# Three weight slabs in place of five for the self-attention keys and values, with the second copies of the keys made by DMA

## What is computed

```python
h = rmsnorm(x, p['norm_mix_pre'][i])
proj = h @ p['w_in_attn'][j]
q, k, v, cq = jnp.split(proj, [Q_WIDTH, Q_WIDTH + KV_WIDTH, Q_WIDTH + 2 * KV_WIDTH], axis=-1)
k = k.reshape(b, l, N_KV_HEADS, HEAD_DIM)      # 3 heads of 64
v = v.reshape(b, l, N_KV_HEADS, HEAD_DIM)
...
s = jnp.einsum('bcqkgd,bcskd->bckgqs', qb, kb).astype(jnp.float32) / math.sqrt(HEAD_DIM)
```

## Time and profile before

| | |
|---|---|
| median of 3 runs | 1857.19 us (1854.53 to 1864.68) |
| the profiled execution | 1860.35 us, span 1858.5 us, mean granted TensorE clock 0.986 |
| TensorE busy | 1757.7 us, 95% of the span |
| VectorE, ScalarE, GpSimd busy | 791.6, 698.7, 749.0 us |
| memory projections of both layers | until 74.6 us |
| slabs 16 to 20 (keys and values) | 74.6 to 106.9 us |
| transposes of the values | 106.9 to 110.1 us |
| four query slabs | 110.1 to 135.8 us |

### The profile page before, as it was taken

One profiled execution on the slowest core, in us unless ns is written; L12 is line 12 of the kernel. 1 busy time (PEld: TensorE's weight loads), 2 busy tenths in 40 slices (PEclk: granted clock), 3 DMA queues, 4 the chain that ended last, 5 costly groups with the idle time before them and its releaser, 6 DMA issues.

```text
span 1858.5 us, 31140 instructions
## 1 busy us (share of the span) xinstructions
PE 1757.7 (95%) x13115; PEld 1683.0 (91%) x13115; DVE 791.6 (43%) x1534; ACT 698.7 (38%) x1318; POOL 749.0 (40%) x438
## 2 busy tenths in 40 slices
PE   6999999999999999999899999989999999999996
PEld 5997887998999999998798989877898999999996
DVE  5427777315412112126856676755504411212124
ACT  6416666324312121224455555553514312122221
POOL 1231121242736354451345555553232745445451
PEclk9999999999999999999899999998999999999998
DMA  5521210121222222221222222212121222222221
GB/s 217 191 80 52 69 64 30 57 87 51 91 84 87 80 80 85 86 80 46 84 88 87 78 94 83 92 60 102 46 80 58 91 80 80 86 85 80 80 87 67
DMA packets 47659, 153.68 MB, mean 83 GB/s; under 512 B 8257, under 2 KB 10017, under 8 KB 47265
## 3 DMA queue, kind: packets, MB, share of 16 engines
q1 hardware_dynamic: 40144, 140.59, 22.3%
q10 hardware_dynamic: 7376, 11.10, 1.8%
HBM read 145.21 MB, written 6.47 MB: 82 GB/s over the span
## 4 chain that ended last, share of the span: by engine, by line
PE 81%; DVE 8%; ACT 4%; POOL 3%; issue 2%; DMA 1%; SPq 0%; POOLq 0%; DVEq 0%; ACTq 0%
PE ps L959 70%; DVE mix L1459 1%; PE ps L942 1%; PE ps L1123 1%; PE ps L1094 1%; POOL sq L2075 1%; ACT dec L856 1%; DVE x L1462 1%; PE ps L1175 1%; PE ps L1112 1%; PE ps L1198 1%; PE ps L1332 1%; POOL w_lo L1954 1%; DVE big_lo L1403 1%; DMA raw<-in_slabs 1%
## 5 line engine op out<-in xcount | busy, mean ns | idle before, releaser
L1954 POOL TENSOR_TENSOR w_lo<-raw,w_hi 128x1024 fp32r<-128x1024 f32 x225 | 547.9, 2437 | 753.3 <-ACT w_hi L472 661.2
L959 PE MATMUL ps<-big_hi,w_hi 128*128 128x288 f32 x3552 | 781.1, 301 | 7.9 <-POOL w_lo L1954 3.2
L959 PE MATMUL ps<-big_lo,w_hi 128*128 128x288 f32 x3552 | 758.9, 297 | 7.7 <-DVE big_lo L1403 7.7
L959 PE MATMUL ps<-big_hi,w_lo 128*128 128x288 f32 x3552 | 765.1, 296 | 0.0
L959 PEld LDWEIGHTS ps<-big_hi,w_hi 128*128 128x128 f32 x3552 | 574.9, 190 | 17.6 <-issue 12.5
L959 PEld LDWEIGHTS ps<-big_lo,w_hi 128*128 128x128 f32 x3552 | 571.3, 189 | 13.1 <-DVE big_lo L1403 12.2
L959 PEld LDWEIGHTS ps<-big_hi,w_lo 128*128 128x128 f32 x3552 | 575.9, 189 | 0.1
L472 ACT ACTIVATE w_hi<-raw 128x1024 fp32r<-128x1024 f32 x242 | 255.3, 1057 | 489.7 <-DMA raw<-in_slabs 479.8
L1713 DVE TENSOR_TENSOR mix<-ps,mix 128x576 f32<-128x576 f32 x62 | 47.0, 758 | 307.3 <-PE ps L959 307.3
L1701 DVE SCALAR_TENSOR_TENSOR relu<-ps,rstd 128x576 f32<-128x576 f32 x60 | 45.4, 757 | 280.2 <-PE ps L959 280.2
L1997 POOL TENSOR_TENSOR hid<-relu 128x576 f32<-128x576 f32 x64 | 98.6, 1543 | 157.6 <-DVE relu L1701 157.5
(11 more groups left out here) (197 smaller groups left out, 1644.6 us busy)
## 6 DMA issues: line engine op xcount, KB each, us to landing
raw<-in_slabs SPq DMA_DIRECT2D x242, 512.0 KB, 3.4
row<-acs_prompt ACTq DMA_DIRECT2D x16, 384.0 KB, 3.3
bias<-in_alibi SPq DMA_DIRECT2D x12, 256.0 KB, 2.7
x<-in_x SPq DMA_DIRECT2D x2, 1152.0 KB, 8.6
out_h<-state ACTq DMA_DIRECT2D x4, 384.0 KB, 2.6
out_y<-x SPq DMA_DIRECT2D x2, 576.0 KB, 2.8
kms<-in_mk SPq DMA_DIRECT2D x2, 512.0 KB, 5.2
vms<-in_mv SPq DMA_DIRECT2D x2, 512.0 KB, 6.3
```

Source lines behind the costliest of these rows:

```text
L959: ins = pe.matmul(ps[:, bank + h, 0:hi_c - lo_c], w[:, s % RING, kt], a[:, k0 + kt, lo_c:hi_c], start=start, stop=stop, skip_group_check=True)
L1954: pool.tensor_tensor(w_lo[:, s % RING], raw[:, s % RING], w_hi[:, s % RING].bitcast(F32), ALU.subtract).then_inc(lo_done, 1)
```

## The change

The three key heads and three value heads of 64 columns are packed into three slabs: keys 0 and 1, key 2 and value 0, values 1 and 2. The arrays in memory stay as they were (five slabs, of which the first three have each key head twice); the first two packed slabs are put together in the ring slot from 64 columns of one slab and 64 of another, each by a DMA of its own (`load_halves`), whose runs are 64 floats long. VectorE evicts the halves separately. The copy of each key head on the other partition half is made by a DMA from `k_all` to `k_all`, issued on the SP queue after a wait on `freed`; TensorE waits for it (`k_moved`) before the first scores of that head, and ScalarE before it stores the keys. The value head 0 is transposed from partitions 64 to 127, with 64 rows.

```diff
--- before.py
+++ after.py
@@ -76,7 +76,8 @@
 
 
 MEM_SLABS = 2 * MEM_W // P
-KV_SLABS = KVH + 2
+KV_SLABS = KVH
+KV_EXTRA = KVH + 2 - KV_SLABS
 Q_SLABS = (Q_W + MEM_W) // P
 OUT_SLABS = 2 * KT
 FF_SLABS = FF_CHUNKS * SLABS_FF
@@ -87,7 +88,8 @@
 CQ_SLABS = MEM_W // P
 ATTN_SLABS = KV_SLABS + Q_SLABS
 SSM_SLABS = 1 + PAIRS * PAIR_SLABS + CQ_SLABS
-ALL_SLABS = 2 * MEM_SLABS + ATTN_SLABS + SSM_SLABS + 2 * (OUT_SLABS + FF_SLABS)
+SLABS = 2 * MEM_SLABS + ATTN_SLABS + SSM_SLABS + 2 * (OUT_SLABS + FF_SLABS)
+ALL_SLABS = SLABS + KV_EXTRA
 
 
 C_MIX_PRE, C_MIX_POST, C_FF_PRE, C_FF_POST, C_MEM = 0, 16, 32, 48, 64
@@ -361,6 +363,8 @@
         mem_arrived, const_in, cache_in = [sem(f"mem_arrived{i}") for i in range(2)], sem("const_in"), sem("cache_in")
         mv_used, vm_done = sem("mv_used"), sem("vm_done")
         vt_done, va_done = sem("vt_done"), sem("va_done")
+        half_in = [sem(f"half_in{i}") for i in range(2)]
+        k_moved = [sem(f"k_moved{i}") for i in range(KVH)]
         bias_in = [sem(f"bias_in{i}") for i in range(2)]
         s_done, biased = sem("s_done"), sem("biased")
         max_done, exp_done, normed = sem("max_done"), sem("exp_done"), sem("normed")
@@ -466,9 +470,11 @@
 
             def split_hi(s):
 
-                if s >= ALL_SLABS:
+                if s >= SLABS:
                     return
                 act.wait_ge(raw_in[s % RING], at(loop, raw_in[s % RING], 16 * (s // RING + 1)))
+                if 0 <= s - 2 * MEM_SLABS < 2:
+                    act.wait_ge(half_in[s - 2 * MEM_SLABS], 16)
                 act.activation(w_hi[:, s % RING], raw[:, s % RING], ACT.Copy).then_inc(hi_done, 1)
 
             def split_to(s):
@@ -640,6 +646,7 @@
                     next_slab()
             n.n += UNITS
 
+            act.wait_ge(k_moved[1], 16)
             act.dma_start(swk_out[:, :, 0:DEC], k_all[0:HD, :, P:P + DEC]).then_inc(stored, 16)
             act.dma_start(swk_out[:, :, DEC:], k_all[0:HD, :, SPAN - P:]).then_inc(stored, 16)
             act.dma_start(swv_out[0:DEC], v_all[0:DEC, 1]).then_inc(stored, 16)
@@ -1061,9 +1068,8 @@
                 if b >= 2:
                     pe.wait_ge(va_done, b - 1)
                 c0, c1 = block_cols(b)
-                for k in range(2):
-                    ins = pe.transpose(ps[0:c1 - c0, S_BANK + b % 2, k * P:(k + 1) * P], v_t[:, k, c0:c1], mats[:, 0])
-                ins.then_inc(vt_done, 1)
+                pe.transpose(ps[0:c1 - c0, S_BANK + b % 2, 0:HD], v_t[HD:, 0, c0:c1], mats[HD:, 0, HD:])
+                pe.transpose(ps[0:c1 - c0, S_BANK + b % 2, HD:HD + P], v_t[:, 1, c0:c1], mats[:, 0]).then_inc(vt_done, 1)
             for j in range(QT):
                 projection()
             g_q = n.g - QT
@@ -1077,6 +1083,8 @@
                 g, j = q // QT, q % QT
                 if u == 0:
                     pe.wait_ge(freed, g_q + q + 1)
+                    if j == 0:
+                        pe.wait_ge(k_moved[g], 16)
                     if t >= 2:
                         pe.wait_ge(biased, n_ - 1)
 
@@ -1538,18 +1546,23 @@
             norm_ready()
 
 
-            for k in range(KVH):
-                b = group()
-                dve.tensor_tensor(k_all[:, k, P:P + HALF], b[:, 0], rstd[:, 1, 0:HALF], ALU.mult)
-                dve.tensor_tensor(k_all[:, k, P + HALF:], b[:, 1], rstd[:, 1, HALF:], ALU.mult).then_inc(freed, 1)
-            for k in range(2):
-                dve.tensor_tensor(halves(v_t[:, k]), group(), halves(rstd[:, 1]), ALU.mult).then_inc(freed, 1)
+            def keys(src, half, g):
+                dve.tensor_tensor(k_all[half, g, P:P + HALF], src[half, 0], rstd[half, 1, 0:HALF], ALU.mult)
+                return dve.tensor_tensor(k_all[half, g, P + HALF:], src[half, 1], rstd[half, 1, HALF:], ALU.mult)
+
+            low, high = slice(0, HD), slice(HD, P)
+            src = group()
+            keys(src, low, 0)
+            keys(src, high, 1).then_inc(freed, 1)
+            src = group()
+            keys(src, low, 2)
+            dve.tensor_tensor(halves(v_t[high, 0]), src[high], halves(rstd[high, 1]), ALU.mult).then_inc(freed, 1)
+            dve.tensor_tensor(halves(v_t[:, 1]), group(), halves(rstd[:, 1]), ALU.mult).then_inc(freed, 1)
             for b in range(BLOCKS):
                 dve.wait_ge(vt_done, b + 1)
                 rows = DEC if b == 0 else P
                 src = ps[0:rows, S_BANK + b % 2, :]
-                dve.tensor_copy(v_all[0:rows, 1 + b, 0:2, :], src[:, 0:P].rearrange("p (h d) -> p h d", h=2))
-                dve.tensor_copy(v_all[0:rows, 1 + b, 2, :], src[:, P + HD:2 * P]).then_inc(va_done, 1)
+                dve.tensor_copy(v_all[0:rows, 1 + b], src[:, 0:KVH * HD].rearrange("p (h d) -> p h d", h=KVH)).then_inc(va_done, 1)
 
             def query_tile(j, dst, sample=None):
 
@@ -2131,17 +2144,19 @@
                     sp.wait_ge(slab_done, at(loop, slab_done, s - RING + 1))
                 sp.dma_start(raw[:, s % RING].rearrange("p k c -> p (k c)"), src).then_inc(raw_in[s % RING], 16)
 
+            extra = [0]
+
             def load_slabs(count, turns=1):
 
                 if turns == 1:
                     for _ in range(count):
-                        load_slab(slabs[n.s], n.s)
+                        load_slab(slabs[n.s + extra[0]], n.s)
                         n.s += 1
                     return
                 loop.per = {"slab_done": count}
                 for i in range(turns):
                     for k in range(count):
-                        src = slabs[bass.ds(i * count + n.s + k, 1)].rearrange("s p c -> (s p) c")
+                        src = slabs[bass.ds(i * count + n.s + extra[0] + k, 1)].rearrange("s p c -> (s p) c")
                         loop.i = i
                         load_slab(src, n.s + k)
                         loop.i = None
@@ -2156,7 +2171,17 @@
             sp.dma_start(x[:, KT // 2:], x_in[:, KT // 2:]).then_inc(x_arrived[1], 16)
             load_slabs(2)
             load_slabs(4, 2)
-            load_slabs(2)
+            def load_halves(first, second, i):
+
+                src = [slabs[2 * MEM_SLABS + t].rearrange("p (k c) -> p k c", k=KT)[:, :, 0:HD] for t in (first, second)]
+                sp.wait_ge(slab_done, n.s - RING + 1)
+                sp.dma_start(raw[:, n.s % RING, :, 0:HD], src[0]).then_inc(raw_in[n.s % RING], 16)
+                sp.dma_start(raw[:, n.s % RING, :, HD:], src[1]).then_inc(half_in[i], 16)
+                n.s += 1
+
+            load_halves(0, 1, 0)
+            load_halves(2, KVH, 1)
+            extra[0] = KV_EXTRA
 
             sp.wait_ge(slab_done, 2 * MEM_SLABS)
             sp.wait_ge(mv_used, 2 * MEM_H)
@@ -2165,11 +2190,17 @@
             load_slabs(2)
             sp.dma_start(kms[:], mk_in[0]).then_inc(kms_in, 16)
             sp.dma_start(vms[:], mv_in[0]).then_inc(kms_in, 16)
-            load_slabs(KV_SLABS + QT - 2)
+            low, high = slice(0, HD), slice(HD, P)
+            for evicted, g, dst, src in ((1, 0, high, low), (1, 1, low, high), (2, 2, high, low)):
+                if g != 1:
+                    load_slabs(1)
+                sp.wait_ge(freed, 2 * MEM_SLABS + evicted)
+                sp.dma_start(k_all[dst, g, P:], k_all[src, g, P:]).then_inc(k_moved[g], 16)
+            load_slabs(KV_SLABS + QT - 4)
             for j in range(2):
                 sp.dma_start(bias[:, j], alibi[j]).then_inc(bias_in[j], 16)
             for q in range(TILES):
-                load_slab(slabs[n.s], n.s)
+                load_slab(slabs[n.s + extra[0]], n.s)
                 n.s += 1
                 if q + 2 < TILES:
                     sp.wait_ge(biased, UNITS_J * (q + 1))
```

## The result

The changed kernel takes 1839.67 us (median of 6 executions, 1833.48 to 1846.4) against 1859.13 us for the kernel before, measured beside it (6 executions, 1848.77 to 1864.68). The ratio is 0.9893 with a 95% interval of 0.9864 to 0.9923. It is faster, as forecast, and by more than forecast: the 13.0 us of the prediction are a ratio of 0.9930, just outside the interval. The time itself lies in the stated range, at its lower end, but against a kernel before that came out 1.9 us slower than the runs the forecast started from.

What follows compares the result with a forecast made beforehand. TensorE, busy for 95% of the span, was taken to bound the kernel, with back-to-back matmuls in the changed stage. Two slabs (12.8 us) plus value transposes (0.2) gave 13.0 us gained, so 1844.2 us; range 1839.5 to 1850.5.

Steps and rivals of the forecast that it cites:

- the 13.0 us of the prediction: Whole kernel: total gain, 12.8 us from two slabs less on TensorE plus 0.2 us from the value transposes.
- the stated range: Whole kernel: time between 1839.5 and 1850.5 us, reaching up to the half-pace loads with their clock loss.
- Two slabs at 6.38 us: Key and value stage on TensorE: two slabs less gain 12.8 us (12.7 to 12.9).
- The cover of the loads in halves, of the evictions and of the key copies: Slabs 16 to 18 and the first scores: all three hidden behind other work, cost 0.
- How the numbers follow: Chances and spread: forecast 0.83; runs 2.7 us below to 7.5 above their median, 1.2 GHz stretches of 1.7 us each.
- The prediction's last sign of being wrong: Loads on time but time outside the range: then clock stretches or later stages did it, against the reading that they move along.
- the value transposes: Gap of 3.25 us before the query slabs: 0.2 us gained, bounds 0 and 0.5, by quicker copies and narrower transposes.
- the packets: Half loads of slabs 16 and 17: 31 ns per 256-byte packet, 5.6 us per slab, 0.9 us to spare for slab 16.
- my bound of 5.1: Key copies from one partition half to the other: at most 5.1 us to landing, over 33 us spare before the scores.
- The first (halves at half the pace): Rival, slabs 16 and 17: loads at 62 ns per packet, 4.4 us late, 1848.6 us, or 1850.3 with clock loss; chance 0.08.
- The second: Rival, loads of slabs 16 and 17: small packets cost as much as large, 38 us late, 1882 us; chance 0.04.
- the third: Rival, first scores: TensorE arrives 13 us early but waits for something keeping its own time, 1857 us; chance 0.05.

Runs made afterwards that it cites:

- the whole loads: The changed kernel with the three slabs packed in memory, slabs 16 and 17 loaded whole, not in halves; ratio 0.9947 to the kernel before.
- the copies alone: The kernel before, still five slabs, with each key head evicted once and its other copy made by a DMA on SP's queue; ratio 1.0001 to the kernel before.
- the values-first order: The kernel with three slabs loaded whole, slabs reordered to begin with values 1 and 2, value transposes between eighths of the last; ratio 0.9865 to the kernel before.

## Why the prediction was right or wrong

**Right: the place and the size of the gain.** Two slabs at 6.38 us, 12.8 us: measured 32.24 - 19.44 = 12.80. The cover of the loads in halves, of the evictions and of the key copies held; the loads and the copies were tested by edits of their own, and the evictions are seen in the chain, which has no wait for them. With the gap it is 12.7 us in the stage. By groups, where the clock's losses are taken off, the change is worth 14.1 us with about 1 us of uncertainty; the 13.0 us of the sum stand at the edge of that. In the traces 0.76 us of the rest lie in the first slab load at 3.07 us, which the change does not touch: it took 8.78 to 8.95 us in the three traces with five slabs and 8.07 to 8.68 in the eight with three. Why stays open, and the prediction had no term for it.

**Wrong: the spread, and with it the number.** The step that failed is the one under "How the numbers follow": that runs differ only by stretches at 1.2 GHz of 1.7 us each, so that a median of a few runs is good to 4 or 5 us and 1857.19 us could be the base. What the runs showed in its place is that each of the two feed-forward parts takes either its slow or its quick course, some 9 us apart, and that a median over three or six executions moves by steps of that size. The prediction's last sign of being wrong is what came: the loads landed on time, and a later stage moved the time.

The three shown runs of the kernel before (1854.53 to 1864.68) hid it: of 73 seen later 42 are shorter than the shortest of these, down to 1836.66. The six beside the change had a mean of 1858.1 us where the 73 have 1852.4; the first six of the changed kernel had 1839.3 where its 16 later ones have 1835.4, so part of this luck cancelled. Over all executions (with the two experiments that neither cost nor gain, the whole loads and the copies alone) the means are 1852.8 us with five slabs (91) and 1837.3 us with three (34), a difference of 15.5 us with a 95% uncertainty of 2.6. That just contains the 13.0, and the 14.1 with ease; of the 19.5 us between the two measured medians some 4 are thus luck of the draw. The forecast of 1844.2 us was too high since its base of 1857.19 was, and the measured 0.9893 lies below the 0.9916 of these means. That the measured median of 1839.67 still fell into the stated range is luck as well: the range was built on stretches of 1.7 us.

**Wrong in size: the value transposes.** I took 0.2 us gained; the gap is 3.37 us for 3.25. A pair now costs 0.24 + 0.26 = 0.50 us where it cost 0.42: the narrower transpose from partitions 64 to 127 is not cheaper in that place. The path is another one, too. Before, each step was one pair on TensorE and two copies on VectorE; now no copy stands in the chain, and each step is two pairs on TensorE, one after the other (0.24 + 0.26 + 0.21 + 0.26 us from 93.56 on). So the quicker copy could save nothing. A step takes 1.05 us (93.56, 94.61) where it took 1.02, and the last pair makes up the rest. Other traces of the three-slab kernels have 3.36 or 3.37 us as well.

**Sized too carefully: the packets.** I took 31 ns per packet of 256 bytes from the earlier trace rows and measured 14. The two halves of slab 16 had landed 4.5 us after the first issue, not 5.6. It decided nothing. The 17 ns of busy time in the earlier trace rows were near it, so the load of that row was probably held up by something else than its packets; no run shows by what. The Trainium skill (DMA: Bandwidth & Descriptors, Specifications) says that below 512 bytes the DMA engine reads, modifies and writes and misses line rate. The loads of 256 bytes ran at up to 291 GB/s here, and a slab in 4 KB runs at 413 in one slice of the same view, so the trace agrees that the small ones miss the full rate; that there is a second access to each packet no run shows.

**A bound that did not hold.** Two of the three key copies took 6.5 us to land, more than my bound of 5.1 from the earlier trace rows; they were under way together with the loads of `kms`, `vms` and a slab, which may be the reason. The last landed by 86.96 + 6.5 = 93.5 us and the scores start at 120.5; 27 us of cover took it.

**The rivals.** The first (halves at half the pace) did not happen, but the runs of 64 bytes showed its mechanism to be real: 3.3 us late, and 1.5 us more in clock right behind the wait, where I had put 1.7. The second and the third did not happen.

## What to carry to other kernels

Where the chain runs through back-to-back matmuls, a removed slab is worth its distance to the next one, to a tenth of a microsecond, and that is read from a handful of rows. Before a forecast is made in per mille, look for courses: several executions and not three, with the clock taken off, and ask whether they fall into groups; a median of few draws from such groups moves by the distance of the groups. Here a load that landed 2 us early cost nothing although it came in halves, and one that was 3.3 us late was paid in full by the wait, and by half as much again in clock. A trace has to be read to its end: in that of the values-first order the 1.2 us gained in the stage were lost behind it, where a slab load took 1.4 us longer to land.

## What the runs showed of the hardware that I had not expected

- The same stream of matmuls (128x128 by 128x288, two passes over the halves) runs at 2.4 GHz in one of two rhythms: 131, 131, 132, 140 ns, mean 133.3, or 129, 131 (in one trace 128, 132) ns, mean 130.0. At 2.4 GHz that is 320 against 312 cycles for 288 columns. It stays for a whole feed-forward part of some 360 us and more, over slab borders, and with an extra matmul at the start of each stage only the slow one was seen (one trace, and 12 executions by their products).
- Half loads of 256-byte runs out of HBM, in rows 512 bytes apart, reached 291 GB/s; the issue of a DMA of 1024 runs of 64 bytes held the SP queue for 0.67 to 1.14 us, with one issue every 0.86 us, against 0.33 us for the quickest issues of 128 runs; that this, and not the packets, was the first limit is likely and not proven.
- A transpose of 64 rows and 64 columns followed by one of 128 took longer than two of 128: 0.50 against 0.42 us for the pair.
